# The last stage's weights take their norm's channel scales inside the split into high and low halves, on ScalarE and DVE, in place of a step of their own on GpSimd

## What is computed

```python
def _rms(x, g):
    xf = x.astype(jnp.float32)
    y = xf * lax.rsqrt(jnp.mean(xf * xf, axis=-1, keepdims=True) + RMS_EPS)
    return (y * g.astype(jnp.float32)).astype(x.dtype)

def _stick_breaking(q, k, v):
    ...
        z = jnp.einsum('bhqd,bshd->bhqs', qb, k).astype(jnp.float32) * scale
        log_beta = jax.nn.log_sigmoid(z)
        log_1mb = jnp.where(mask, jax.nn.log_sigmoid(-z), 0.0)
        suffix = lax.cumsum(log_1mb, axis=3, reverse=True) - log_1mb
        a = jnp.where(mask, jnp.exp(log_beta + suffix), 0.0)
        return jnp.einsum('bhqs,bshe->bhqe', a.astype(v.dtype), v)
```

## Time and profile before

| | |
|---|---|
| time, median of 3 runs | 3027.35 us (3024.14 to 3033.77) |
| the profiled execution: time, span | 3027.2 us, 3025.4 us |
| PE, matmul | 2927.3 us busy, 97% |
| PE, weight loads | 2441.1 us, 81% |
| DVE | 1499.7 us, 50% |
| ACT | 1069.9 us, 35% |
| POOL | 819.0 us, 27% |
| chain of work that ended last | PE 90%, DVE 4%, POOL 2%, ACT 2% |
| the last stage's turns | 2720 to 2796, 2796 to 2872, 2872 to 2936 us |

### The profile page before, as it was taken

One profiled execution on the slowest core, in us unless ns is written; L12 is line 12 of the kernel. 1 busy time (PEld: TensorE's weight loads), 2 busy tenths in 40 slices (PEclk: granted clock), 3 DMA queues, 4 the chain that ended last, 5 costly groups with the idle time before them and its releaser, 6 DMA issues.

```text
span 3025.4 us, 35873 instructions
## 1 busy us (share of the span) xinstructions
PE 2927.3 (97%) x14832; PEld 2441.1 (81%) x14832; DVE 1499.7 (50%) x2055; ACT 1069.9 (35%) x1664; POOL 819.0 (27%) x446
## 2 busy tenths in 40 slices
PE   7999999899999999999999899999999999989989
PEld 6888888789888888888888789888888787777777
DVE  5554345454455534554345454455533666557653
ACT  3322234344333322332234444333223344344332
POOL 2000145364300001000145464300004544355432
PEclk8999999999999999999999999999999999999999
DMA  4332232133233232332332133233232211122111
GB/s 128 98 98 91 91 92 63 49 112 112 84 98 98 88 104 94 100 96 93 101 86 63 56 112 112 84 106 97 88 99 79 63 57 59 54 71 63 56 56 49
DMA packets 301362, 257.21 MB, mean 85 GB/s; under 512 B 10871, under 2 KB 299536, under 8 KB 301200
## 3 DMA queue, kind: packets, MB, share of 16 engines
q1 hardware_dynamic: 300880, 254.90, 27.2%
q0 software_dynamic: 320, 0.03, 0.0%
HBM read 252.79 MB, written 2.10 MB: 84 GB/s over the span
## 4 chain that ended last, share of the span: by engine, by line
PE 90%; DVE 4%; POOL 2%; ACT 2%; issue 1%; DMA 1%; SPq 0%; ACTq 0%; POOLq 0%; DVEq 0%
PE PS L1417 28%; PE PS L1419 27%; PE PS L1418 27%; PE PS L1423 2%; PE PS L1659 2%; POOL WL L2628 1%; PE PS L1664 1%; DVE WL L2119 1%; DVE AF L2534 1%; ACT WH L1772 1%; POOL SC L2636 0%; PE PS L1615 0%; PE PS L1506 0%; DMA SC<-in_consts_dram 0%; PE PS L1609 0%
## 5 line engine op out<-in xcount | busy, mean ns | idle before, releaser
L1417 PE MATMUL PS<-XH,WL 128*128 128x512 f32 x2256 | 903.8, 401 | 16.0 <-issue 8.9
L1419 PE MATMUL PS<-XH,WH 128*128 128x512 f32 x2256 | 885.5, 393 | 0.0
L1418 PE MATMUL PS<-XL,WH 128*128 128x512 f32 x2256 | 884.6, 392 | 0.0
L1772 ACT ACTIVATE WH<-RAW 128x1024 fp32r<-128x1024 f32 x448 | 465.7, 1044 | 1032.6 <-PE PS L1419 1001.0
L2119 DVE TENSOR_TENSOR WL<-RAW,WH 128x1024 fp32r<-128x1024 f32 (+1 forms) x296 | 388.1, 1314 | 496.9 <-ACT WH L1772 495.7
L2628 POOL TENSOR_TENSOR WL<-RAW,WH 128x1024 fp32r<-128x1024 f32 x184 | 445.1, 2427 | 477.1 <-ACT WH L1772 446.1
L1417 PEld LDWEIGHTS PS<-XH,WL 128*128 128x128 f32 x2256 | 427.7, 190 | 98.6 <-issue 15.7
L1419 PEld LDWEIGHTS PS<-XH,WH 128*128 128x128 f32 x2256 | 426.9, 189 | 92.6
L1418 PEld LDWEIGHTS PS<-XL,WH 128*128 128x128 f32 x2256 | 427.8, 190 | 81.8 <-issue 0.5
L1417 PE MATMUL PS<-AR,WL 128*128 128x512 f32 (+1 forms) x1216 | 469.2, 386 | 24.7 <-DVE AR L2364 7.5
L2636 POOL TENSOR_TENSOR SC<-SC 128x512 f32<-128x512 f32 x70 | 114.5, 1636 | 1315.0 <-ACT SC L1796 1310.3
(11 more groups left out here) (245 smaller groups left out, 3265.7 us busy)
## 6 DMA issues: line engine op xcount, KB each, us to landing
RAW<-in_w_ffn_gu_dram SPq DMA_DIRECT2D x176, 512.0 KB, 3.5
RAW<-in_w_ffn_down_dram SPq DMA_DIRECT2D x80, 512.0 KB, 3.4
RAW<-in_w_mix_in_dram SPq DMA_DIRECT2D x48, 512.0 KB, 3.8
RAW<-in_w_xkv_dram SPq DMA_DIRECT2D x32, 512.0 KB, 3.3
RAW<-in_a_w_in_dram SPq DMA_DIRECT2D x32, 512.0 KB, 4.0
RAW<-in_w_mix_out_dram SPq DMA_DIRECT2D x16, 512.0 KB, 3.5
RAW<-in_w_xq_dram SPq DMA_DIRECT2D x16, 512.0 KB, 3.3
RAW<-in_w_xo_dram SPq DMA_DIRECT2D x16, 512.0 KB, 3.3
```

The costliest lines, as they stand in the source:

```text
L1417: pe.matmul(o, ll, rh, start=start, stop=False, skip_group_check=skip)
L1418: pe.matmul(o, lh, rl, start=False, stop=False, skip_group_check=skip)
L1419: return pe.matmul(o, lh, rh, start=False, stop=stop, skip_group_check=skip)
L1772: act.activation(h, src, ACT.Copy).then_inc(sg["wh"].up(n))
```

## The change

Units with channel scales lose their scale step on POOL. Their split on ACT becomes one activation for each k tile, with the tile's column of GA as the scale (WH = high half of RAW x GA), and their low half on DVE one scalar_tensor_tensor for each k tile (RAW x GA less WH). As `on_dve` now says yes for all such units, the low halves of the eight k strips go from POOL to DVE. In numbers: 32 steps on POOL and 8 low halves on POOL go; 24 strips have 8+8 operations of 128x128 in place of 1+1 of 128x1024, and 8 halves of v have 4+4 operations of 128x256.

```diff
     def on_dve(self, n):
         key, _, gain, kind = self.units[n]
         if gain is not None:
-            return key[0][1][0] != "k"
+            return True
         return kind == "w" and STAGES[key[0][0]].startswith("ffn")
...
             def split(n):
                 _, _, g0, kind = units[n]
-                if g0 is None:
-                    on.wait_ge(*raw_ready(n))
+                on.wait_ge(*raw_ready(n))
...
                 else:
-                    on.wait_ge(*sg["wg"].at(n))
-                    act.activation(h, src, ACT.Copy).then_inc(sg["wh"].up(n))
+                    for k in range(src.shape[1]):
+                        t = act.activation(h[:, k, :], src[:, k, :], ACT.Copy, scale=GA[:, g0 + k:g0 + k + 1])
+                    t.then_inc(sg["wh"].up(n))
...
             def low(n):
                 if P.on_dve(n):
                     h, l = w_slot(n)
+                    w, g0 = raw_slot(n), units[n][2]
                     on.wait_ge(*sg["wh"].at(n))
-                    dve.tensor_tensor(l, raw_slot(n), F(h), ALU.subtract).then_inc(sg["wl"].up(n))
+                    if g0 is None:
+                        t = dve.tensor_tensor(l, w, F(h), ALU.subtract)
+                    else:
+                        for k in range(w.shape[1]):
+                            t = dve.scalar_tensor_tensor(l[:, k, :], w[:, k, :], GA[:, g0 + k:g0 + k + 1], F(h[:, k, :]), ALU.mult, ALU.subtract)
+                    t.then_inc(sg["wl"].up(n))
...
-            def scale(n):
-                g0 = units[n][2]
-                w = raw_slot(n)
-                nk, nc_ = w.shape[1], w.shape[2]
-                on.wait_ge(*raw_ready(n))
-                pool.tensor_tensor(w, w, GA[:, g0:g0 + nk].unsqueeze(2).to_broadcast([128, nk, nc_]), ALU.mult).then_inc(sg["wg"].up(n))
```

More of the change, by code:

```diff
@@ L118, in __init__ @@
         self.splitting = False
-        self.halves, self.scales, self.clock = [], [], 0
+        self.halves, self.clock = [], 0
         self.held, self.turn, self.soon, self.empties, self.watch = set(), [], [], {}, lambda n: None
@@ L141, in add @@
                 self.low()
[L142 to L148, removed]
     def low(self):
@@ L274, in pump @@
                 self.add("load", (n,))
-                if self.units[n][2] is not None:
-                    self.scales.append((n, self.clock + 14))
                 moved = True
@@ L287, in pump @@
                     pad = ("pad",) if self.units[n][3] == "pad" else ()
-                    while self.scales and self.scales[0][0] <= n:
-                        self.scale()
                     self.add("split", (n,), *pad, "wh")
@@ L2720, in bmul @@
                 pool.tensor_tensor(b, b, OM[n % 2][:, :, T - N + 1:T + 1], ALU.mult).then_inc(sg["gprob"].up(s, n))
-            do = {"setup2": setup2, "tables": tables, "split": split, "scale": scale, "low": low, "sq": sq, "sq2": sq2, "norm_a": norm_a, "norm2a": norm2a,
+            do = {"setup2": setup2, "tables": tables, "split": split, "low": low, "sq": sq, "sq2": sq2, "norm_a": norm_a, "norm2a": norm2a,
                   "barrier": barrier, "mpv": mpv, "mn": mn, "cb2": cb2, "ny_a": ny_a, "mem_a": mem_a, "dn": dn, "dsin": dsin,
```

## The result

The changed kernel takes 3054.48 us (median of 4 runs, 3054.24 to 3058.56) beside 3030.56 us for the kernel before (4 runs, 3024.14 to 3034.51): the ratio of the means is 1.0084, 95% interval 1.0062 to 1.0106, so slower. Forecast were 3046 us and a range of 3023 to 3066. The profiled execution took 3054.6 us, its span 3052.8 us.

The account below looks back on a forecast made before the run. TensorE, busy 97%, was taken to bound the kernel, with last-stage waits ending on DVE. Turns +11.1, +7.0, +4.0 and start -2.7 gave +19.4 on 3027.2, so 3046 us; own range 3037 to 3055, with rivals 2 and 3 3023 to 3066.

Parts of the forecast that it names:

- turn A: Last stage's first head-pair turn, 2720 to 2796 us: +11.1 us, of which 4.5 at its start, 2.7 k strip, 3.9 second half.
- turn B: Second head-pair turn, to 2872 us: +7.0 us, of which 2.0 at its start, 1.1 k strip, 3.9 second half.
- turn C: Third head-pair turn, to 2936 us: +4.0 us, as 2.0 at its start, 1.5 k strip, 0.5 later.
- High and low halves: Per strip, ScalarE's high halves take 2.4 us (+1.35), DVE's low halves 2.2 us (+1.0, or +2.2 for k).
- Rival 3: Small operations do not overlap: +11 us over some ten places, two more clock drops +6; 3063 us, chance 0.22.
- The start: Start of last stage: norm's power step 3.0 us sooner, giving -0.7 at a short wait and -2.0 through the mask, together -2.7.
- The turns' chains: In three head-pair turns, longer splits and low halves ahead of L2541 delay TensorE: +11.1, +7.0 and +4.0 us.
- The clock: Half-rate clock after waits over 3 us: costed at nothing, two drops more or fewer, each about 3 us, in the range.
- Rival 1: The lock decides: longer splits and low halves hide in DVE's idle time, only freed scans count; 3012 us, chance 0.1.
- Rival 2: They cancel: TensorE has 1 to 2 us more slack per place, half of +22 us goes; 3030 us, chance 0.18.
- What was to show it: Signs: steps near 0.29 and 0.26 us, scan pairs 2.3 us, first wait 1.3, transposes' L2541 waits from 13.4 to over 30.

Follow-up runs that it names:

- e1: Kernel before without the GpSimd factor steps, scales left out of the last stage's weights, nothing else changed; ratio to the kernel before 0.9953.
- e5: e1 with the k strips' low halves on DVE, every high and low half one operation; ratio to the kernel before 0.9947.
- e3: Kernel before with only DVE's low halves (q, g, v) made by k tile, multiplied by one, k's still on GpSimd; ratio to the kernel before 1.0054.
- e6: e5 with the high halves made by k tile with their scale, low halves still one operation; ratio to the kernel before 1.0011.
- e9: The change with low halves of units with scales 8 instead of 4 ticks behind their split; ratio to the kernel before 1.0051.
- e10: The change with low halves of units with scales 10 instead of 4 ticks behind their split; ratio to the kernel before 1.0044.

## Why the prediction was right

**The sum, by its own places.** Growth of the distance between the two kernels' transposes (the change less before, from the start of the stretch), beside the terms of the prediction; times are those of the kernel before:

| place | predicted | measured |
|---|---|---|
| up to the first scores, 2698.1 | -2.7 | -1.6 |
| from there to turn A | 0 | +1.3 |
| turn A: 2724.5, 2729.9, 2735.0 | 2.5, 2.0, 2.7 | 2.5, 1.9, 2.9 |
| turn A, second half | 3.9 | 7.0 |
| turn B: 2794.6 with 2803.2; 2810.9 | 2.0; 1.1 | 1.5; 0.2 |
| turn B, second half | 3.9 | 4.2 |
| turn C | 2.0 + 1.5 + 0.5 | 1.4 + 0.5 + 0.2 |
| behind turn C | 0 | 0.8 |
| sum | +19.4 | +22.8 |

- **High and low halves: right.** 2.44 us a strip forecast at 2.4, 1.70 a half of v at 1.7; 2.19 forecast at 2.2, 1.66 at 1.7. The reading of the long chains with 0.09 us overlap held. The Trainium skill (VectorE: DVE Perf Modes, The DRAIN you can't avoid), taken as no overlap, gives 8 x 0.350 = 2.8 us for a strip; 2.19 measured speak against it, as the chain of four did. But the same section adds that an operation that is not held starts earlier, which I had left out; with that the trace agrees. Rival 3 falls with that.
- **The start: the mechanism held, its addition did not.** The power step came at once, the transposes behind it 0.8 us sooner (0.7 forecast). The mask's DMA was issued 2.2 us sooner (1.9 forecast), in the stretch's time, but it landed only 1.6 us sooner, and the first scores follow it. I had added 0.7 and 2.0; the later of two conditions sets the end, so only the mask's share counts. The wait of L1648 is 2.6 us and not 1.3: the 0.8 us came back in it.
- **The turns' chains: right** to 0.2 us at each of A's first three transposes, and 0.3 to 1.0 us too high at each place of B and C but B's second half, which is 0.3 too low.
- **The clock: the step that failed.** I cost it at nothing, since I expected as many waits near 3 us as before. The turns of the change have ten waits of 2.3 to 2.9 us and five windows at 0.50 of some 3.4 us; before they had two waits over 4 us and two windows of some 6.8. H is 38.1 us against 32.0, so +3.1 us net, nearly all of the 3.4 us by which the sum was short; that it comes so close is in part luck, since the start and B and C miss the sum by 1 to 2 us each, in both directions. A window more or less fits most of these: one twice as long ahead of turn A (+1.3 where I had 0), and in B and in C 3.4 us at 0.50 where 6.8 were. It fits that A's second half took 7.0 us: two of its windows at 0.50 (2775.7 and 2786.0) lie there, 3.4 us of cost together. The third (2731.4) is not seen in the sum: TensorE has to wait for L2536 behind it anyway, at 2738.52. And "nothing" hid two large terms: the removed steps give back 9.9 us of clock (e1), and the new halves take more than that again. The size was right within the range only because they cancel.
- **Rival 1 (the lock decides, 3012 us)** is what happens without the small operations: e1 and e5 have 3016.47 and 3018.03 us. Its point of decision, a strip's low half under 1.4 us and its split under 1.3, is not met by 2.2 and 2.4. **Rival 2** falls with +22.8; its sum was wrong too: half of 22 us less 2.7 is +8, 3035.5 us and not 3030.
- **What was to show it:** steps of 0.29 us for high and 0.26 for low halves, yes (16 take 4.79 and 4.28 us, 8 take 2.44 and 2.19); scans of 512 at 2.33 us a pair, yes; L2536 waits over 30 us in more than nine places, yes (32.1 in 16), new ones at those of 2724 and 2735, now 2731.22 (2.31 us) and 2746.46 (2.67), and at 2795, now 2815.97 (2.77); the first wait at 1.3, no (2.6).

## What to carry to other kernels

An engine that is half idle can still set the end, if its order is fixed: ask of each added operation which later one stands behind it there, and who waits for that. Splitting one operation in eight for the sake of a per-row scale doubles its time and, beside GpSimd, lets it be held more than once; look first whether the scale can go somewhere smaller, here onto x (0.9949 instead of 1.0084). And when parts are tested apart, test them on both sides: the high halves cost 6.5 us on one base and 16.4 on the other.

## What was not expected of the hardware

- A strip of eight low halves, 2.19 us alone, took 5.26 us beside two GpSimd operations and 6.39 beside three (e3), where a single low half of 1.2 us took at most 3.07 in the kernel before. Yet all low halves together were held no longer than before.
- The half clock can double the price of waits: from the kernel before to e1, the waits changed by 9.6 us and the clock's share by 9.9. It isn't proportional, though: from e5 to e6 it is 3.6 us on 13.4, and e9 to e10 has less waiting (by 2.7 us) and more time at 0.50 (by 7.5), which stays unexplained.
- The mask's DMA of 64 KB, issued 2.2 us sooner, took 0.6 us longer to reach its reader; what it met on the way was not tried.
